# A two-block network on one core: the column sums of the norms taken from a running sum on VectorE, and two layer norms' means taken tile by tile

## What is computed

```python
def _rmsnorm(x, g):
    xf = x.astype(jnp.float32)
    y = xf * lax.rsqrt(jnp.mean(xf * xf, axis=-1, keepdims=True) + EPS) * g.astype(jnp.float32)
    return y.astype(x.dtype)

def layer_norm(x, g, b):
    xf = x.astype(jnp.float32)
    mu = jnp.mean(xf, -1, keepdims=True)
    var = jnp.mean(jnp.square(xf - mu), -1, keepdims=True)
    return ((xf - mu) * lax.rsqrt(var + LN_EPS) * g.astype(jnp.float32) + b.astype(jnp.float32)).astype(x.dtype)
...
# first block, each sub-layer; mod = silu(c) @ ada_w + ada_b
h = _rmsnorm(x, norm_g[l, 0]) * (1.0 + mod[:, 0, 1]) + mod[:, 0, 0]
x = x + 0.5 * mod[:, 0, 2] * _swiglu(h, ffn_w_gate[l, 0], ffn_w_up[l, 0], ffn_w_down[l, 0])
...
# second block, each sub-layer
x = layer_norm(DEEPNORM_ALPHA * x + (1.0 + g_m) * y, ln_mix_g[i], ln_mix_b[i])
```

## Time and profile before

| what | us |
|---|---|
| median of 3 runs | 3610.05 |
| lowest and highest | 3609.8, 3616.33 |
| the profiled execution, its own time | 3612.29 |
| its span in the trace | 3610.20 |
| PE busy | 3281.6 (91%) |
| DVE busy | 981.8 (27%) |
| ACT busy | 451.5 (13%) |
| DMA, mean over the span | 203 GB/s |
| mean granted clock of TensorE | 0.942 of full speed |

### The profile page before, as it was taken

The page is one execution under the profiler, slowest core; times in us unless marked ns, Lnnn a source line. Parts: engine busy times, 40 slices in busy tenths (PEclk is TensorE's granted clock), DMA queues, the critical chain, the costliest instruction groups (busy, mean ns, idle before and its releaser), DMA issues.

```text
span 3610.2 us, 55645 instructions
## 1 busy us (share of the span) xinstructions
PE 3281.6 (91%) x23870; PEld 2765.2 (77%) x23871; DVE 981.8 (27%) x2054; ACT 451.5 (13%) x1029; POOL 18.6 (1%) x27
## 2 busy tenths in 40 slices
PE   3999999899899999989999878997879999999997
PEld 3887888778788888877888767886868776678874
DVE  5203221240130222323114342358421111111112
ACT  1000022100000001211000200002511111011110
POOL 0000000000000000000000000000000000000000
PEclk7999999999999998999999869999589999999999
DMA  8645533265274463335536303770127788888884
GB/s 333 237 175 208 209 113 128 105 245 201 106 276 175 178 230 128 115 113 219 218 134 235 141 0 135 286 291 24 49 87 300 286 313 310 325 343 326 323 313 177
DMA packets 55178, 732.10 MB, mean 203 GB/s; under 512 B 6576, under 2 KB 6760, under 8 KB 10516
## 3 DMA queue, kind: packets, MB, share of 16 engines
q1 hardware_dynamic: 51092, 716.69, 52.4%
q0 software_dynamic: 3968, 13.74, 1.1%
HBM read 729.32 MB, written 4.23 MB: 203 GB/s over the span
## 4 chain that ended last, share of the span: by engine, by line
PE 75%; DVE 10%; DMA 10%; issue 3%; ACT 2%; DVEq 0%; SPq 0%; POOL 0%; ACTq 0%; POOLq 0%
PE psum L617 44%; PE psum L994 10%; PE psum L1034 8%; DMA ring<-in_up_dram 4%; DVE ring L1347 3%; DMA ring<-in_up_e_dram 3%; PE psum L665 2%; DMA ring<-in_w_qk_dram 2%; DVE work L1778 1%; PE psum L793 1%; PE psum L1011 1%; PE psum L1050 1%; PE psum L677 1%; DVE rms L1405 1%; DVE h_t L1421 1%
## 5 line engine op out<-in xcount | busy, mean ns | idle before, releaser
L617 PE MATMUL psum<-h_t,ring 128*128 128x256 f32 x6336 | 1402.1, 384 | 124.6 <-DMA ring<-in_up_dram 64.6
L617 PEld LDWEIGHTS psum<-h_t,ring 128*128 128x128 f32 x6336 | 1215.1, 193 | 312.2 <-issue 133.2
L617 PE MATMUL psum<-work,ring 128*128 128x256 f32 x2752 | 604.9, 383 | 26.3 <-ACT work L1188 6.8
L617 PEld LDWEIGHTS psum<-work,ring 128*128 128x128 f32 x2752 | 527.6, 192 | 103.2 <-issue 16.4
L994 PE MATMUL psum<-h_t,ring 128*64 128x96 f32 x11264 | 468.7, 246 | 8.4 <-DMA ring<-in_up_e_dram 6.8
L994 PEld LDWEIGHTS psum<-h_t,ring 128*64 128x64 f32 x11264 | 465.4, 137 | 11.8 <-issue 11.8
L1034 PE MATMUL psum<-ring,work 128*96 128x512 f32 x704 | 304.0, 593 | 7.6 <-DVE work L2060 7.6
L1347 DVE SCALAR_TENSOR_TENSOR ring<-ring,cond 128x1024 f32<-128x1024 f32 x240 | 279.3, 1221 | 26.7 <-DMA ring<-in_ada_dram 18.3
L1034 PEld LDWEIGHTS psum<-ring,work 128*96 128x96 f32 x704 | 114.1, 163 | 192.2 <-issue 189.9
L1382 DVE TENSOR_TENSOR work<-work,psum 128x256 f32 (+1 forms) x126 | 53.1, 421 | 673.8 <-PE psum L617 658.9
L2060 DVE TENSOR_TENSOR work<-work,psum 128x256 f32 x176 | 74.2, 421 | 401.8 <-PE psum L994 401.8
(11 more groups left out here) (306 smaller groups left out, 1683.6 us busy)
## 6 DMA issues: line engine op xcount, KB each, us to landing
ring<-in_up_e_dram SPq DMA_DIRECT2D x64, 2048.0 KB, 7.6
ring<-in_ada_dram SPq DMA_DIRECT2D x60, 2048.0 KB, 8.1
ring<-in_up_dram SPq DMA_DIRECT2D x55, 2048.0 KB, 8.6
ring<-in_down_e_dram SPq DMA_DIRECT2D x32, 1792.0 KB, 7.5
ring<-in_down_dram SPq DMA_DIRECT2D x20, 2816.0 KB, 10.5
ring<-in_up_e_dram SPq DMA_DIRECT2D x32, 1536.0 KB, 8.3
ring<-in_down_e_dram SPq DMA_DIRECT2D x16, 2048.0 KB, 8.0
ring<-in_w_qk_dram SPq DMA_DIRECT2D x12, 2048.0 KB, 9.7
```

The costliest lines, as they stand in the source:

```text
L617: mm = pe.matmul(half(b), w, moving(k, j * lin.groups + m), start=(k == 0), stop=(k == depth - 1))
```

## The change

In an RMS norm, DVE adds the squares of tiles 0 to 6 together as they come, into tile 0 of `h_t` (`squares_so_far`). The six additions stand in `add_to_x` of the product ahead, each before DVE's wait for the next tile; for the first norm they stand behind the `ada` sums at the start of the program. PE multiplies two tiles by ones: the running sum, then tile 7.

In `ln0` and `ln1` DVE does the same with `x` itself into `rms` (`x_so_far`), and PE sums `rms` and tile 7. In `ln2` and `ln3` PE still adds eight tiles, but waits for each on its own (`x_summed` becomes a counted signal). The second sum of a layer norm, over the squares, keeps its eight products.

```diff
             def norm(p):
                 pe.wait_ge(bank_free[5], reads(p, 5))
-                for k in range(DT):
-                    pe.wait_ge(signal["squares"], p.of("squares", k + 1))
-                    mm = pe.matmul(half(5), ones[:, :], h[:, k, :], start=(k == 0), stop=(k == DT - 1))
-                mm.then_inc(signal["full5"], 1)
+                pe.wait_ge(signal["most_squares"], p.of("most_squares", 1))
+                pe.matmul(half(5), ones[:, :], h[:, 0, :], start=True, stop=False)
+                pe.wait_ge(signal["squares"], p.of("squares", DT))
+                pe.matmul(half(5), ones[:, :], h[:, DT - 1, :], start=False, stop=True).then_inc(signal["full5"], 1)
+
+            def mean(p):
+
+                pe.wait_ge(bank_free[5], reads(p, 5))
+                if "most_x" in p.what:
+                    pe.wait_ge(signal["most_x"], p.of("most_x", 1))
+                    pe.matmul(half(5), ones[:, :], rms[:, :], start=True, stop=False)
+                    for b in range(LIN):
+                        pe.wait_ge(bank_free[b], reads(p, b))
+                    pe.matmul(half(5), ones[:, :], x[:, DT - 1, :], start=False, stop=True).then_inc(signal["full5"], 1)
+                else:
+                    for b in range(LIN):
+                        pe.wait_ge(bank_free[b], reads(p, b))
+                    for k in range(DT):
+                        pe.wait_ge(signal["x_summed"], p.of("x_summed", k + 1))
+                        mm = pe.matmul(half(5), ones[:, :], x[:, k, :], start=(k == 0), stop=(k == DT - 1))
+                    mm.then_inc(signal["full5"], 1)
...
-            def add_to_x(p, scale):
+            def squares_so_far(p, f):
+
+                dve.wait_ge(signal["squares"], p.of("squares", f + 1))
+                e = dve.tensor_tensor(h[:, 0, :], h[:, 0, :], h[:, f, :], ALU.add)
+                if f == DT - 2:
+                    e.then_inc(signal["most_squares"], 1)
+                else:
+                    e.then_inc(dve_done, steps.one())
+                    dve.wait_ge(dve_done, steps.count())
+
+            def x_so_far(p, f):
+
+                e = dve.tensor_tensor(rms[:, :], x[:, 0, :] if f == 1 else rms[:, :], x[:, f, :], ALU.add)
+                if f == DT - 2:
+                    e.then_inc(signal["most_x"], 1)
+                else:
+                    e.then_inc(dve_done, steps.one())
+                    dve.wait_ge(dve_done, steps.count())
+
+            def add_to_x(p, scale, after):
 
                 lin = p.what
                 for j in range(lin.chunks):
                     for m in range(lin.groups):
                         f, b = j * lin.groups + m, lin.at[j][m][0]
+                        if f > 1 and "most_squares" in after.what:
+                            squares_so_far(after, f - 1)
+                        elif f > 1:
+                            for k in range(LIN):
+                                dve.wait_ge(bank_free[k], reads(after, k) - 2 + (k < f) + (k + 4 < f))
+                            x_so_far(after, f - 1)
                         dve.wait_ge(*group_end(p, j, m, 0, p.slot(j)))
...
             ada_next(p, 0, ada_b(0))
+            for f in range(1, DT - 1):
+                squares_so_far(place("norm0", 0), f)
...
                 b = down.what.at[j][m][0]
+                if f > 1:
+                    for k in range(LIN):
+                        dve.wait_ge(bank_free[k], reads(place("ln1"), k) - 2 + (k < f) + (k + 4 < f))
+                    x_so_far(place("ln1"), f - 1)
...
             for f in range(DT):
                 dve.scalar_tensor_tensor(x[:, f, :], y_t[:, f, :], mod1[:, 2 * DT + f:2 * DT + f + 1],
-                                         x[:, f, :], ALU.mult, ALU.add).then_inc(dve_done, steps.one())
-            dve.wait_ge(dve_done, steps.count())
-            dve.sem_inc(x_summed, 1)
+                                         x[:, f, :], ALU.mult, ALU.add).then_inc(signal["x_summed"], 1)
```

More of the change, by code:

```diff
@@ L168, in stages @@
     down = lambda src: Linear(4, 2, 44 * P, src)
-    norm = with_(uses(b5=1), squares=DT, root=1, h=DT)
+    norm = with_(uses(b5=1), squares=DT, most_squares=1, root=1, h=DT)
     ln = with_(uses(b5=1, b6=1), mean=DT, squares=DT, root=1, h=DT)
+    ln_after = with_(ln, most_x=1)
+    ln_along = with_(ln, x_summed=DT)
     logits = with_(uses(b4=4, b5=4), maxima=1, probs=HG, bias_in=16)
@@ L621, in linear @@
                 walk(p, loop, chunk)
-            def over_features(b, src):
-                for k in range(DT):
-                    mm = pe.matmul(half(b), ones[:, :], src[:, k, :], start=(k == 0), stop=(k == DT - 1))
-                mm.then_inc(signal[f"full{b}"], 1)
             def norm(p):
                 pe.wait_ge(bank_free[5], reads(p, 5))
-                for k in range(DT):
-                    pe.wait_ge(signal["squares"], p.of("squares", k + 1))
-                    mm = pe.matmul(half(5), ones[:, :], h[:, k, :], start=(k == 0), stop=(k == DT - 1))
-                mm.then_inc(signal["full5"], 1)
-            def layer_norm(p, between=None):
-                for b in range(LIN):
-                    pe.wait_ge(bank_free[b], reads(p, b))
-                if p.name in ("ln2", "ln3"):
-                    pe.wait_ge(x_summed, 1 if p.name == "ln2" else 2)
-                pe.wait_ge(bank_free[5], reads(p, 5))
-                over_features(5, x)
+                pe.wait_ge(signal["most_squares"], p.of("most_squares", 1))
[17 more added lines that the diff above has]
+                    mm.then_inc(signal["full5"], 1)
+            def layer_norm(p, between=None):
+                mean(p)
                 if between:
@@ L1582, in _ @@
                 ada_next(on("up0"), 0, ada_b(1, l))
-                add_to_x(on("down0"), gate)
+                add_to_x(on("down0"), gate, on("norm1"))
                 take_first(on("norm1"), 1, False)
@@ L1618, in _ @@
                 ada_next(on("up2"), 0, ada_b(3, l))
-                add_to_x(on("down2"), gate)
+                add_to_x(on("down2"), gate, place("norm0", at(l, 1, 1)))
             p = place("final_norm")
```

17 lines of the change are left out of this document (7 added, 10 removed).

## The result

| | median us | lowest to highest | runs |
|---|---|---|---|
| before, in the same comparison | 3616.02 | 3609.80 to 3619.61 | 6 |
| with the change | 3586.57 | 3579.17 to 3593.15 | 6 |

The ratio is 0.9923, with a 95% interval from 0.9906 to 0.9940: 27.8 us of 3616, between 22 and 34. The forecast was 3591.9 and a gain of 18.2; the time lies in the range, near its lower end. So the sign and most of the size are right, and some 10 us more were gained in this comparison than the sum says. Where these come from is the question of all that follows.

A forecast was written before the change was run, and what follows sets the result against it. It took the chain of waits, three quarters PE's, as the bound, with norms where PE stands still. Terms 8.3 + 0 - 2.9 + 3.1 + 4.7 + 4.7 + 0.3 = 18.2 off the 3610.05 median gave 3591.9 us, range 3585 to 3600.

The forecast's parts named there:

- Norms behind a product: `norm1` and `norm2` of both layers and `final_norm`: root starts 1.66 us earlier, limited by ACT's table load; 8.3 us in all.
- the bound of 1.9: Norms behind a product: gain of 1.9 us each if ACT's table load were out of the way.
- `norm0` of layer two: Norm after the layer loop's jump back: DVE's stalls, not PE, make it late, so 0 us gained.
- The second rival: `norm0` of layer two: twelve new instructions remove DVE's second stall, 4.1 us more gained, 3587.8 us; chance 0.28.
- `norm0` of layer one: First norm: six chained additions of 0.46 us now stand in DVE's way; -2.9 us, from -2.1 to -3.1.
- `ln0`, `ln2`, `ln3`, `ln1`: Layer norms: PE's first sum ends earlier, gaining 3.1, 4.7, 4.7 and 0.3 us in this order.
- the lower bound: `ln2` and `ln3`: gain of 3.0 us each if PE stayed at the low clock.
- A microsecond in a norm is a microsecond of the kernel: Stages behind norms: DVE's `ada` sums, transfer and PE's products all move with the norm, so its saving carries through fully.
- The clock: Behind norms and in second sums of `ln0`, `ln1`: idler PE loses clock, costing 7 x 1.7 = 11.9 us, 3603.8; chance 0.08.
- Transfers hide it: Stages behind the norms wait for weights, so the five times 1.66 us are gone: 3600.2 us; chance 0.06.
- The sum not ready: Norms behind a product: DVE's last addition lies on the path, costing 5 x 0.46 = 2.3 us, 3594.2; chance 0.05.
- Slower through the experts' jumps: Experts' loop: longer DVE code makes seven returns stall 3.4 to 4.1 us each, 3620.6 us at 4.1; chance 0.03.

The follow-up runs named there:

- The runs with memsets: Kernel before plus tiny DVE memsets at the start, ahead of the layers' loop: twelve gave ratio 0.9985 to before; six had one execution, 3614.60 us.
- the one with the head at 53: Changed kernel with the first norm's six additions moved to DVE's wait at the program's start; loop's head at DVE instruction 53; ratio 0.9933 to before.
- the two series of the changed kernel: The changed kernel against before, first comparison and an unchanged repeat: ratios 0.9923 and 0.9934, together 0.9930.
- the fillers: Ten overwritten products behind each RMS norm's second product, on the changed kernel with early additions and one memset: ratio 0.9921 to before, its base 0.9926.

## Why the prediction was right, and where not

**Norms behind a product.** Right in place, reason and size: 1.67 where 1.66 was said, and the root sits on the end of the table load in every one. One thing is closer than the working had it: the last product takes 0.70 + 0.03 and not 0.60, so DVE's scaled sum is there at 303.17, 0.1 before the table. With the table load out of the way some 0.1 would be gained by these rows, and not the 0.24 that the bound of 1.9 holds.

**`norm0` of layer two.** The step that failed: "0 us by the rows". The earlier trace rows were read as a stall that stays with the code around it; they show only that nothing the profile knows was waited for. The second rival had the mechanism, the twelve instructions and the 4.1 us, and was given 0.28. The runs with memsets and the one with the head at 53 show it to be right to the instruction. The argument against it, that PE has a jump at the same place, could decide nothing: PE waits for DVE there in any case. This is most of what the sum lacked, 4.2 of the 7.2 us by which the two series of the changed kernel (25.4) exceed 18.2. The forecast itself lies outside the interval of these two series (21.6 to 29.2); the range of 3585 to 3600 holds the result not least because it took in this rival. There is luck in that too: the kernel before took 3616.02 us beside the changed one, 6.0 more than the median that the forecast started from; 27.8 us below that median would be 3582.3, outside the range.

The Trainium skill (Runtime: NRT & Kernel Launch, "Instruction fetch mechanics") says that code comes in blocks, that the next one is loaded ahead of need, and that a taken branch breaks this. The traces agree, with 2.8 to 3.7 us for what the jump goes to (thirteen profiles) and 4.1 to 4.6 more (five) when, by that rule, the next block begins six or twelve instructions behind it. How large a block is, and that the stall is the loading itself, no run here shows.

**`norm0` of layer one.** Predicted -2.9, measured -3.1: 2.73 for the six additions, as 6 x 0.46 says, and two products of 1.22 and 1.06, of which DVE waited for 0.79; the 0.1 allowed for the low clock was 0.3. The other value, 0.35 an addition as L1464 has it without waits, would have been 2.1 for the six. It would follow if, as the Trainium skill (VectorE: DVE Perf Modes, the section on the DRAIN you can't avoid) says, the semaphores cost nothing extra. The row says 2.73, so in a chain where each waits for the one before, the wait has its price.

**`ln0`, `ln2`, `ln3`, `ln1`.** Right within 0.2. In `ln2` and `ln3` PE was at full clock, the value taken and not the lower bound; in `ln1` the sum fell together with S5's transposes as described:

```profile
2480.26 1.06 PE L636 MATMUL psum<-rms,ones 128*128 128x256 f32 x2
...
2481.11 1.06 PE L639 MATMUL psum<-x_t,ones 128*128 128x256 f32 x2
```

Two products of 1.06 stand in place of 4.10, which is the change's gain here. From one and the same step of DVE's tables (L1778 at 2460.97 in before, L1813 at 2439.80) to S5's first product it was 53.08 us and is now 52.53; one more addition of 0.46 stands ahead of that step, so 0.1 is left.

**A microsecond in a norm is a microsecond of the kernel.** It held in the sum, with scatter of one to two microseconds in single stages: the projections behind the first `norm1` gained 1.6 us more than the norm gave them, since PE waited 4.9 us for their chunks in before (1.40, 0.18, 1.64 and 1.69) and 2.5 after (0.74, 1.16 and 0.63).

**The other rivals.** The clock: the low stretch behind the norms did become longer. Behind the first `norm1` it is 16.29 us for 64 instructions where it was 15.70, and the granted clock was 0.50 from 306 to 311, more than the 3.5 us that the prediction named as this rival's sign; behind all of `norm1` and `norm2` of both layers the 64 took 3.9 us more in the profile after than in that of before. Over more profiles it is less: the first 60 instructions behind these norms took 14.5 to 16.1 us with the old order of the RMS norms (24 restarts, 15.0 in the mean) and 14.4 to 16.0 with the new one (28 restarts, 15.4). And the fillers show that even the full 1.3 is mostly hidden by the weights. So the rival's premise holds in part, some 0.4 us a restart on PE, and its price of 1.7 does not. Transfers hide it: no. The sum not ready: no, PE's first product runs at once behind the last group, and the next wait is for ACT. Slower through the experts' jumps: none of the seven returns shows a stall on DVE, before or after.

**What was not foreseen** is how far single executions differ in work that no edit touches. That the first comparison shows 27.8 and its two profiles 31.7 is partly luck of this kind. Six of the seven terms of the sum were right to 0.2 us, and yet one profile of each kernel gave 31.7. The places add up to 21.8, the two series to 25.4 with an interval of 21.6 to 29.2. The remaining 3.6 us can hardly be told from none, and no place of the traces has them.

## What to carry to other kernels

Work out a norm as a chain for its last tile, and then ask for the next thing that is late: here it was the table load, within 0.1 us of the next one. A stall that the profile puts down to "issue" behind a loop's jump can belong to a place in the code and not to the instruction behind it, as it did here; a few instructions more or less ahead of the loop then move it or remove it, and can make an edit look better or worse than it is. Compare two profiles stage by stage and look for jumps where nothing was edited before believing their difference.

## What the runs showed of the hardware

- DVE's jump back in the layers' loop costs 2.8 to 3.7 us, and another 4.1 to 4.6 in front of instruction 54 when the head is 42 or 48; with the head at 53 both are one stall of 7.71. Twelve empty instructions, ahead of the loop, were worth 5.4 us (1.8 to 9.0).
- TensorE's granted clock falls to 0.50 in the middle of a row of equal products in a mix (a pair from 0.39 to 0.63 us), in other mixes from one execution to the next. Such a stretch of 17 us costs 6.6 us, one of 7 us 2.9, and without fillers they came to 2.8 to 17.6 us per execution. This is one source of the scatter between executions; it is not the only one, since two profiles of the changed kernel with 2.8 and 12.3 had spans of 3578.5 and 3577.3 on two chips. Whether products that compute nothing, in the gaps ahead, delay and shorten it, one profile can't show.
- Ten products of filler (20 instructions) in a wait of 4.09 us kept the clock at 1.00 for PE's restart, and yet brought nothing that can be told from none (0.5 us over the four stages); in the projections the wait for weights took it back. The Trainium skill (TensorE: Matmul & The Clock Gate, "Why this matters for your kernels") asks for no longer gaps between bursts of products; the granted clock agrees (0.50 behind a wait of 4.09, 1.00 behind one of 1.86), the time of this kernel hardly depends on the clock at this place.
